# Indirect gathers and scatters that skip empty slots, in a mixture-of-experts kernel on one core

## The chip, the cores and the metric

The kernel runs on 1 core of one Trainium2 chip. The metric is the device time of the whole program in microseconds (us). The engines are named PE (matmul), DVE (vector), ACT (scalar), POOL (GpSimd) and SP (sync, which here only issues transfers). PEld is PE's weight load. All transfers of the core run on the same 16 DMA engines; those that SP issues stand on queue q1, those that POOL issues on queue q0.

## The reference, cut to what matters

One encoder layer on 768 tokens (a sequence of 512 and one of 256) of width 1024, all in float32: a token mixer (differential attention beside retention), then a mixture of experts, then a last RMSNorm. What the change touches is the mixture:

```
e_sel  = top-2 experts of each token, inside its best group      # 32 experts, 768 * 2 = 1536 assignments
h      = silu(x @ w1[e]) * (x @ w3[e])                           # x: 1024, h: 512
y      = h @ w2[e]
out[t] = x2[t] + gate[t, 0] * y[t, 0] + gate[t, 1] * y[t, 1]     # then RMSNorm
```

## The kernel before

The token mixer and the router run in the first 705 us. The router counts the tokens of each expert and cuts each expert's list into blocks of 64 slots (`CAP`). Every expert has at least one block, so there are 32 blocks and one more for each full 64 that an expert exceeds. In this run there are 41 (the groups of the block loop count 41 in the profile). Blocks of one expert follow each other, `served[b]` is the expert of block b, and `nb` is the number of blocks, known only when the router has run. Slots that no token fills stay empty: 41 * 64 = 2624 slots stand for 1536 assignments.

`idxt[p, b]` is an integer that says which half row (512 numbers, 2 KB) partition p of block b wants. Partitions 0 to 63 hold the first halves of the block's 64 rows, partitions 64 to 127 the second halves. It is made by twelve small matmuls (L799) of a slot matrix `Rt` with `Bt`, whose entries are the token's number, and then 2 * token + half (L1537). An empty slot sums to token 0, so it fetches row 0.

The block loop runs on five engines, each in its own program order, joined by semaphores. In block b:

- **POOL** copies column b of `idxt` to `idxb` (L1671), waits for that copy and issues an indirect gather of 128 half rows from `xn_scratch` to the one buffer `xg` (L1674), then waits until `ystage` holds the result of an older block and issues two plain stores of 64 half rows to `y_scratch` (L1681). In its loop the order is gather(b + 2), store(b), then gather(b + 3) and so on, in one queue of instructions.
- **PE** waits for the gather and transposes `xg` to columns (L810), does the down projection of the block before (L841, 16 matmuls), transposes the hidden values (L829), and does the up projection (L820, 32 matmuls).
- **DVE** copies the transposed rows out of PSUM (L1555), forms the hidden values (L1561, L1563) and, when the next block has another expert, copies that expert's w1 and w3 from `rawe` to `cur13a` and `cur13b` (L1577).
- **ACT** does the sigmoid (L1115), copies the result to `ystage` (L1126) after the wait for the older stores, copies the hidden columns (L1120), and, for another expert, copies w2 to `cur2` (L1142).
- **SP** loads the experts' weights into a double buffer (L502), three transfers of 2 MB for each expert: w1 and w3 when DVE has copied the expert two back, w2 when ACT has.

After the last block POOL waits for all stores and issues twelve indirect gathers of 128 rows of 4 KB from `y_scratch` by slot number, two for each tile of 128 tokens (L1698). DVE adds them, scaled by the gates, to `x2` (L1597, L1599), ACT squares and sums (L1152), and the last norm follows (L1155, L1606 on DVE for three tiles, L1705 on POOL for three), then the output stores (L529).

Much earlier, POOL zeroes a small tile and writes the slots of `y_scratch` behind the 32nd block with zeros (L1653), and stores the normalised rows of each tile to `xn_scratch` (L1662).

Of the kernel before, what the change touches and what calls it, by code (L numbers as in the profile page):

```python
# [23 lines left out]
P = 128  # L24
# [15 lines left out]
MAXB = T // CAP  # L40
NOV = (2 * T) // (CAP + 1)
NB = NE + NOV
EW = 12288
EPS = 1e-6
LAM_INIT = 0.8 - 0.6
# [13 lines left out]
_n = 0  # L59
for _name, _w in (("ident", P), ("tri", P), ("ones", P), ("rel", RELW), ("cosA", 32), ("sinA", 32),  # L60
                  ("cosR", 128), ("sinR", 128), ("ecap", NE), ("grank", NG), ("erank", NE),
                  ("iota", P), ("half", 1), ("thr", MAXB - 1), ("tok", NT)):
    _c[_name] = (_n, _n + _w)
    _n += _w
NCST = _n
# [2 lines left out]
def constants():  # L68

    import numpy as np  # L70
    t = np.zeros((P, NCST), np.float32)

    def put(name, v):
        a, b = _c[name]
        t[:, a:b] = v
    i = np.arange(P)
    put("ident", np.eye(P))
    put("tri", (i[:, None] < i[None, :]).astype(np.float32))
    put("ones", 1.0)
# [12 lines left out]
    put("iota", np.arange(P))  # L92
    put("thr", CAP * np.arange(1, MAXB))
    put("half", (i // CAP)[:, None])
    put("tok", i[:, None] + P * np.arange(NT)[None, :])
    return t


def hybrid_layer(nc, A):
# [50 lines left out]
    nbi = small("nbi", [1, 1], I32)  # L150
    served = small("served", [1, NB + 1], I32)
    bcol = small("bcol", [P, 8])
    idxb = small("idxb", [P, 1], I32)
    sdum = small("sdum", [P, 1])
    F_O = off[0]
    FREE = 212800 - F_O
# [6 lines left out]
    zrow = at("zrow", F_O + 36 * KB, [P, 256])  # L163
# [56 lines left out]
    xg = at("xg", D_O + 40 * KB, [P, 512])  # L220
    ystage = at("ystage", D_O + 44 * KB, [P, 512])

    ya = [[at(f"ya{t}{k}", RAW_O + (2 * t + k) * 4 * KB, [P, D]) for k in range(2)] for t in range(NT)]
# [10 lines left out]


    z_d = nc.dram_tensor("z_scratch", [T, D_IN], F32, kind="Internal").ap()
    xn_d = nc.dram_tensor("xn_scratch", [T, D], F32, kind="Internal").ap()
    xn_halves = xn_d.rearrange("t (h n) -> (t h) n", h=2)
    y_d = nc.dram_tensor("y_scratch", [NB * CAP, D], F32, kind="Internal").ap()

    def sem(name):
        return ctx.enter_context(nc.semaphore(name))
    with ctx:
# [100 lines left out]
        s_ys = sem("s_ys")  # L344
        s_md = sem("s_md")
        s_zr = sem("s_zr")
        s_g1 = [sem(f"s_g1{t}") for t in range(NT)]
        s_c2 = sem("s_c2")
        s_sq3 = sem("s_sq3")
# [40 lines left out]
        def _(sp):  # L390
# [90 lines left out]
                    sp.wait_ge(s_lo, ZP + p - 5)  # L481
                    p_piece(p)
            sp.wait_ge(s_mgd, 2 * NT)
            sp.wait_ge(s_ys, 32)
            sp.dma_start(g2[:, :], A["ffn_norm_g"].partition_broadcast(P)[:, 0, :]).then_inc(s_rp, 16)
            sp.dma_start(wrt[:, :, 0:NG], A["w_rg"][0].rearrange("(p c) g -> p c g", c=KC)).then_inc(s_rp, 16)
            for g in range(NG):
# [370 lines left out]
        def _(act):  # L858
# [273 lines left out]
            with act.Fori(1, nb) as b:  # L1132
# [26 lines left out]
        def _(dve):  # L1159
# [377 lines left out]
            link(dve.tensor_scalar(idxt[:, :], ps[4][:, 0:NB + 1], 2.0, C("half"), ALU.mult, ALU.add))  # L1537
            dve.sem_inc(s_nb, 1)

            dve.wait_ge(s_re, 3)  # L1540
# [52 lines left out]
                rsqrt(a, b, D, link)  # L1593
                dve.sem_inc(s_rstd3, 1)
            for t in range(NT):
                dve.wait_ge(s_g1[t], 32)
                link(dve.scalar_tensor_tensor(out=x2[:, t, :], in0=ya[t][0][:, :], scalar=gates[:, 0, t:t + 1],  # L1597
                                              in1=x2[:, t, :], op0=ALU.mult, op1=ALU.add))
                dve.scalar_tensor_tensor(out=x2[:, t, :], in0=ya[t][1][:, :], scalar=gates[:, 1, t:t + 1],  # L1599
                                         in1=x2[:, t, :], op0=ALU.mult, op1=ALU.add).then_inc(s_c2, 1)  # L1600
                if t == 2:
                    last_norm(0, 2)
# [8 lines left out]
        def _(pool):  # L1611
# [34 lines left out]
            silu_steps(1)  # L1646


            pool.memset(zrow[:, :], 0.0).then_inc(s_zr, 1)
            pool.wait_ge(s_zr, 1)  # L1650
            rest = y_d[NE * CAP:NB * CAP, :].rearrange("(e r) (q c) -> (r q) e c", r=32, c=256)
            for u in range(2):
                pool.dma_start(rest[:, u * NOV:(u + 1) * NOV, :],  # L1653
                               zrow[:, :].unsqueeze(1).to_broadcast([P, NOV, 256])).then_inc(s_ys, 16)

            pool.wait_ge(s_hi, ZP + 1)
            pool.tensor_tensor(elo[P_LO[0]][:, :], raw[3][:, :], ehi[P_HI[0]][:, :].bitcast(F32),
                               ALU.subtract).then_inc(s_lo, 1)

            for t in range(NT):  # L1660
                pool.wait_ge(s_rr, t + 1)
                pool.dma_start(xn_d[t * P:(t + 1) * P, :], rrow[t % 2][:, :]).then_inc(s_rst[t % 2], 16)  # L1662

            for k in range(2):
                pool.wait_ge(s_rst[k], 16 * NT // 2)
            pool.wait_ge(s_nb, 1)
            nb = pool.value_load(nbi[0:1, 0:1], min_val=NE, max_val=NB)

            def gather(b):
# [2 lines left out]
                pool.wait_ge(s_ic, b + 1)  # L1672
                pool.sem_inc(s_idx, 1)
                pool.indirect_dma_start(out=xg[:, :], out_offset=None, in_=xn_halves,  # L1674
                                        in_offset=bass.IndirectOffsetOnAxis(ap=idxb[:, 0:1], axis=0)).then_inc(s_gx, 16)

            def store(b):

                pool.wait_ge(s_yc, b + 2)
                for u in range(2):  # L1680
# [9 lines left out]
                gather(b + 2)  # L1690
                store(b)
            store(nb - 1)
            pool.wait_ge(s_ys, 32 * nb + 32)
            pool.wait_ge(s_gx, 16 * nb + 16)
            pool.sem_inc(s_md, 1)
            for t in range(NT):
                for k in range(2):
                    pool.indirect_dma_start(out=ya[t][k][:, :], out_offset=None, in_=y_d,  # L1698
                                            in_offset=bass.IndirectOffsetOnAxis(ap=sloti[:, k, t:t + 1], axis=0)
                                            ).then_inc(s_g1[t], 16)  # L1700

            pool.wait_ge(s_gf, 16)
            for t in range(3):
                pool.wait_ge(s_ym, t + 1)
# [26 lines left out]
```

## Time and profile before

| | |
|---|---|
| median of 3 runs | 1406.74 us (1406.67 to 1407.38) |
| the profiled execution's own time | 1407.34 us |
| its span in the profile | 1405.4 us |
| granted TensorE clock, mean | 0.911 |
| block loop, first gather to last store | 705.56 to 1359.4 us |
| blocks, and blocks that begin another expert | 41, 31 |

The profiled execution agrees with the runs that were timed within 0.6 us. Its span is 1.94 us shorter than its own time, and what lies outside the span is not touched here. The page gives busy shares over the whole span; the block loop takes nearly half of it.

### The profile page before, as it was taken

The page shows a single profiled execution, that of the slowest core. Times are in us where ns is not written, and L with a number is a line of the kernel's source. Part 1 is how long each engine was busy: PE and PEld are TensorE (multiplying, and loading weights), DVE is VectorE, ACT ScalarE, POOL GpSimd, SP SyncE. Part 2 cuts the span into 40 slices and gives each one's busy share as a digit, 9 for nine tenths or more (in the row PEclk, how much of TensorE's full clock was granted, in tenths as well). Part 3 has the DMA queues.
Part 4 walks back from the last instruction along what each step waited for, and adds up shares of the span by engine and source line. Part 5 has one row for each costly group of instructions (what it writes and reads, how often), then busy time and mean ns, then how long its engine had stood idle before and what let it go on. Part 6 is the DMA issues. An engine that isn't in the chain of part 4 may idle for free.

```text
span 1405.4 us, 15836 instructions
## 1 busy us (share of the span) xinstructions
PE 1167.4 (83%) x5178; PEld 697.0 (50%) x5178; DVE 520.6 (37%) x889; ACT 424.7 (30%) x671; POOL 194.0 (14%) x293
## 2 busy tenths in 40 slices
PE   2999999999899779999567888778888888978840
PEld 2788888888666458888522332222233323322210
DVE  3531111115277575643623433333222322234407
ACT  4422222221355563321402233222122121222322
POOL 0011010101070010000011111111111111211134
PEclk9999999999999679999678999999899998999975
DMA  7233332511605045323948999999856587489935
GB/s 278 86 138 112 105 112 107 199 45 48 235 2 173 0 151 182 91 77 142 424 163 322 397 422 421 422 421 422 335 215 238 189 334 277 140 329 422 378 100 214
DMA packets 74047, 311.51 MB, mean 222 GB/s; under 512 B 12576, under 2 KB 12576, under 8 KB 49440
## 3 DMA queue, kind: packets, MB, share of 16 engines
q1 hardware_dynamic: 57824, 258.15, 46.8%
q0 software_dynamic: 16192, 52.97, 10.8%
q8 instruction: 17, 0.28, 0.1%
q14 instruction: 14, 0.11, 0.0%
HBM read 272.29 MB, written 38.80 MB: 221 GB/s over the span
## 4 chain that ended last, share of the span: by engine, by line
PE 63%; DMA 16%; issue 7%; DVE 6%; ACT 4%; POOL 1%; POOLq 1%; SPq 0%; DVEq 0%; ACTq 0%
DMA xg<-xn_scratch,idxb 15%; PE ps L841 13%; PE ps L537 11%; PE ps L539 11%; PE ps L538 11%; PE ps L820 6%; PE ps L810 3%; PE ps L636 1%; ACT ystage L1126 1%; PE ps L657 1%; PE ps L669 1%; PE ps L754 1%; POOL y_scratch L1681 1%; PE ps L648 1%; DVE att L1291 1%
## 5 line engine op out<-in xcount | busy, mean ns | idle before, releaser
L841 PE MATMUL ps<-cur,hT 128*64 128x512 f32 x656 | 191.6, 738 | 4.3 <-ACTq L1145 4.3
L537 PE MATMUL ps<-whi,xTh 128*128 128x512 f32 x480 | 188.5, 393 | 6.2 <-DVE xTl L1228 4.1
L538 PE MATMUL ps<-wlo,xTh 128*128 128x512 f32 x480 | 187.9, 391 | 0.0
L539 PE MATMUL ps<-whi,xTl 128*128 128x512 f32 x480 | 187.8, 391 | 0.0
L1555 DVE COPY xT<-ps 128x512 f32<-128x512 f32 x41 | 28.4, 692 | 422.7 <-PE ps L810 422.7
L820 PE MATMUL ps<-cur13a,xT 128*64 128x512 f32 x656 | 154.2, 612 | 6.2 <-DVEq L1579 5.4
L820 PE MATMUL ps<-cur13b,xT 128*64 128x512 f32 x656 | 148.1, 592 | 0.0
L1172 DVE TENSOR_TENSOR wlo<-raw,whi 128x2048 fp32r<-128x2048 f32 x27 | 61.7, 2292 | 218.2 <-ACT whi L864 218.0
L810 PE MATMUL ps<-cst,xg 128*128 128x128 f32 x168 | 35.9, 345 | 106.5 <-DMA xg<-xn_scratch,idxb 106.4
L1681 POOL DMA_DIRECT2D y_scratch<-ystage x82 | 54.4, 665 | 499.5 <-ACT ystage L1126 498.5
L1126 ACT ACTIVATE ystage<-ps 128x512 f32<-128x512 f32 x41 | 24.5, 598 | 309.8 <-PE ps L841 309.8
L1142 ACT ACTIVATE cur<-rawe 128x4096 f32 x31 | 112.2, 3619 | 0.0
L841 PEld LDWEIGHTS ps<-cur,hT 128*64 128x64 f32 x656 | 53.4, 168 | 113.5 <-issue 110.2
L915 ACT ACTIVATE zst<-ps 128x512 f32<-128x512 f32 x60 | 35.8, 598 | 235.1 <-PE ps L539 235.1
L537 PEld LDWEIGHTS ps<-whi,xTh 128*128 128x128 f32 x480 | 90.8, 189 | 25.4 <-ACT xTh L884 6.8
L539 PEld LDWEIGHTS ps<-whi,xTl 128*128 128x128 f32 x480 | 90.8, 189 | 19.1
L538 PEld LDWEIGHTS ps<-wlo,xTh 128*128 128x128 f32 x480 | 90.8, 189 | 18.9
L810 PEld LDWEIGHTS ps<-cst,xg 128*128 128x128 f32 x168 | 25.3, 211 | 142.2 <-DMA xg<-xn_scratch,idxb 140.6
L820 PEld LDWEIGHTS ps<-cur13b,xT 128*64 128x64 f32 x656 | 50.1, 137 | 90.7 <-issue 90.7
L820 PEld LDWEIGHTS ps<-cur13a,xT 128*64 128x64 f32 x656 | 47.3, 140 | 83.1 <-issue 78.7
L1615 POOL DMA_DIRECT2D z_scratch<-zst x60 | 33.2, 553 | 333.0 <-ACT zst L915 332.9
L1577 DVE COPY cur13a<-rawe 128x4096 f32 x31 | 71.3, 2301 | 7.9 <-issue 7.9
(219 smaller groups left out, 1470.6 us busy)
## 6 DMA issues: line engine op xcount, KB each, us to landing
rawe<-in_w SPq DMA_DIRECT2D x96, 2048.0 KB, 12.1
raw<-in_w_in SPq DMA_DIRECT2D x20, 1024.0 KB, 5.8
z_scratch<-zst POOLq DMA_DIRECT2D x60, 256.0 KB, 2.3
y_scratch<-ystage POOLq DMA_DIRECT2D x82, 128.0 KB
gat<-z_scratch SPq DMA_DIRECT2D x12, 512.0 KB, 4.0
y_scratch<-zrow POOLq DMA_DIRECT2D x2, 2944.0 KB
raw<-in_w_out SPq DMA_DIRECT2D x4, 1024.0 KB, 7.1
xn_scratch<-rrow POOLq DMA_DIRECT2D x6, 512.0 KB, 2.9
```

What stands on the lines that cost most here:

```text
L537: pe.matmul(out, ah, bh, start=first, stop=False)
L538: pe.matmul(out, ah, bl, start=False, stop=False)
L539: return pe.matmul(out, al, bh, start=False, stop=last)
L810: mm = pe.transpose(ps[2][:, c * P:(c + 1) * P], xg[:, c::4], ident)
L820: mm = pe.matmul(ps[0][u * CAP:(u + 1) * CAP, :], xT[:, c, h * CAP:(h + 1) * CAP], cur13[h][:, :, c * 512 + u * 256:c * 512 + u * 256 + 25 ...
L841: mm = pe.matmul(ps[6][u * CAP:(u + 1) * CAP, :], hT[:, k, h * CAP:(h + 1) * CAP], cur2[:, c:c + 512], start=(h == 0 and k == 0), stop=(h ...
L915: act.activation(zst[k][:, :], ps[k][:, :], ACT.Copy).then_inc(s_zev, 1)
L1126: act.activation(ystage[:, :], ps[6][:, :], ACT.Copy).then_inc(s_yc, 1)
L1142: act.activation(cur2[:, :], rawe[:, bass.ds((e % 2) * EW + 4 * PIECE, 2 * PIECE)], ACT.Copy).then_inc(s_cw2, 1)
L1172: dve.tensor_tensor(elo[slot][:, :], raw[slot_raw][:, :], hi[:, :].bitcast(F32), ALU.subtract).then_inc(s_lo, 1)
L1577: dve.tensor_copy(cur13[h][:, :, :], pair[:, :, h * PIECE:(h + 1) * PIECE]).then_inc(s_c13, 1)
L1681: pool.dma_start(y_d[bass.ds(b * CAP, CAP), u * 512:(u + 1) * 512], ystage[u * CAP:(u + 1) * CAP, :]).then_inc(s_ys, 16)
```

## The change

Three things change together. First, the code in `Bt` is now such that a filled slot of block b gives the index 4 * token + 2 * choice + half (at most 3071), while an empty slot gives 4096 or 4097. The gather passes `bounds_check=4 * T - 1` and `oob_is_err=False`, so that it moves nothing for empty slots. For the index to fit, `xn_scratch` holds each row twice, once for each choice. Second, the result of a block is stored by one indirect scatter with the same indices, straight to row (token, choice) of `y_scratch`, where it was two plain stores to the block's place. The scatter needs its own copy of the index column, `idxs`. Third, the twelve indirect gathers at the end become six plain transfers of 1 MB, issued by SP. What belongs to it: the zeroing of unused slots and SP's wait on it go away, `xg` is zeroed once, and ACT's first loop step is taken out of its loop, so that the wait counts stay constant where they must.

```
-    xn_d = nc.dram_tensor("xn_scratch", [T, D], F32, kind="Internal").ap()
-    y_d = nc.dram_tensor("y_scratch", [NB * CAP, D], F32, kind="Internal").ap()
+    xn_d = nc.dram_tensor("xn_scratch", [T, 2, D], F32, kind="Internal").ap()
+    xn_halves = xn_d.rearrange("t k (h n) -> (t k h) n", h=2)
+    y_d = nc.dram_tensor("y_scratch", [T, 2, D], F32, kind="Internal").ap()
+    y_halves = y_d.rearrange("t k (h n) -> (t k h) n", h=2)
...
@@ sync, router's inputs
-            sp.wait_ge(s_ys, 32)
@@ sync, after the weights
             sp.wait_ge(s_md, 1)
+            for t in range(NT):
+                sp.dma_start(ya[t][:, :, :], y_d[t * P:(t + 1) * P, :, :]).then_inc(s_g1[t], 16)
@@ scalar, rows_out
-                act.wait_ge(s_ys, 32 * b + 32)
+                if not (isinstance(b, int) and b == 0):
+                    act.wait_ge(s_ys, 16 * b)
...
-            rows_out(nb - 1)
+            last = act.value_load(nbi[0:1, 1:2], min_val=NE - 1, max_val=NB - 1)
+            rows_out(last)
@@ vector, router
-                                  C("tok")[:, t:t + 1], ALU.is_equal, ALU.mult).then_inc(s_tb, 1)
+                                  C("code")[:, q:q + 1], ALU.is_equal, ALU.mult).then_inc(s_tb, 1)
+            link(dve.tensor_scalar(nbi[:, 1:2], run[0:1, a, Z0 + NE - 1:Z0 + NE], float(NE - 1), None, ALU.add))
...
-            link(dve.tensor_scalar(idxt[:, :], ps[4][:, 0:NB + 1], 2.0, C("half"), ALU.mult, ALU.add))
+            link(dve.tensor_scalar(idxt[:, :], ps[4][:, 0:NB + 1], -2.0, C("half"), ALU.mult, ALU.add))
@@ gpsimd
-                pool.dma_start(xn_d[t * P:(t + 1) * P, :], rrow[t % 2][:, :]).then_inc(s_rst[t % 2], 16)
+                pool.dma_start(xn_d[t * P:(t + 1) * P, :, :], rrow[t % 2][:, :].unsqueeze(1).to_broadcast([P, 2, D])).then_inc(s_rst[t % 2], 16)
...
+            pool.memset(xg[:, :], 0.0).then_inc(s_zr, 1)
+            pool.wait_ge(s_zr, 1)
             pool.wait_ge(s_nb, 1)
@@ gather
-                                        in_offset=bass.IndirectOffsetOnAxis(ap=idxb[:, 0:1], axis=0)).then_inc(s_gx, 16)
+                                        in_offset=bass.IndirectOffsetOnAxis(ap=idxb[:, 0:1], axis=0),
+                                        bounds_check=4 * T - 1, oob_is_err=False).then_inc(s_gx, 16)
@@ store
                 pool.wait_ge(s_yc, b + 2)
-                for u in range(2):
-                    pool.dma_start(y_d[bass.ds(b * CAP, CAP), u * 512:(u + 1) * 512],
-                                   ystage[u * CAP:(u + 1) * CAP, :]).then_inc(s_ys, 16)
+                pool.tensor_copy(idxs[:, :], idxt[:, bass.ds(b, 1)]).then_inc(s_is, 1)
+                pool.wait_ge(s_is, b + 2)
+                pool.sem_inc(s_ids, 1)
+                pool.indirect_dma_start(out=y_halves,
+                                        out_offset=bass.IndirectOffsetOnAxis(ap=idxs[:, 0:1], axis=0),
+                                        in_=ystage[:, :], in_offset=None,
+                                        bounds_check=4 * T - 1, oob_is_err=False).then_inc(s_ys, 16)
@@ end
-            for t in range(NT):
-                for k in range(2):
-                    pool.indirect_dma_start(out=ya[t][k][:, :], out_offset=None, in_=y_d, ...
```

## Rows read from the trace of the kernel before

**Rows 1.** The page: bandwidth in 40 equal slices, and the chain's shares.

```profile
GB/s 278 86 138 112 105 112 107 199 45 48 235 2 173 0 151 182 91 77 142 424 163 322 397 422 421 422 421 422 335 215 238 189 334 277 140 329 422 378 100 214
...
PE 63%; DMA 16%; issue 7%; DVE 6%; ACT 4%; POOL 1%; POOLq 1%; SPq 0%; DVEq 0%; ACTq 0%
```

**Rows 2.** Who waited for whom, in total us, times, longest us.

```profile
PE ps L810 <- DMA xg<-xn_scratch,idxb: 106.4, 31, 7.6
...
POOL idxb L1671 <- DVEq L1538: 27.7, 1, 27.7
```

**Rows 3.** The chain in order of time: start us, length us, what.

```profile
908.45 6.97 DMA xg<-xn_scratch,idxb
916.32 5.15 PE ps L841 x16
924.98 6.88 DMA xg<-xn_scratch,idxb
```

**Rows 4.** POOL in order of time, 889 to 925 us; idle before in brackets.

```profile
889.27 1.91 POOL L1681 DMA_DIRECT2D y_scratch<-ystage  x2 [11.55 <-ACT ystage L1126]
...
906.33 1.12 POOL L1681 DMA_DIRECT2D y_scratch<-ystage  x2 [13.13 <-ACT ystage L1126]
907.44 0.20 POOL L1671 COPY idxb<-idxt 128x1 int32 x1
908.45 1.01 POOL L1674 DMA_INDIRECT xg<-xn_scratch,idxb  x1 [0.81 <-POOL idxb L1671]
```

**Rows 5.** DVE in order of time, beside the first of these stores.

```profile
888.26 2.29 DVE L1577 COPY cur13b<-rawe 128x4096 f32 x1
```

**Rows 6.** The block loop's groups, 705 to 1357 us.

```profile
L1681 POOL DMA_DIRECT2D y_scratch<-ystage x80 | 53.3, 668 | 489.2 <-ACT ystage L1126 488.3
L1674 POOL DMA_INDIRECT xg<-xn_scratch,idxb x42 | 42.3, 1007 | 35.7 <-POOL idxb L1671 33.5 <-issue 2.3
```

**Rows 7.** The instructions of xg: time to landing.

```profile
DMA to landing us min/median/max: 3.1/6.9/7.9
```

**Rows 8.** PE in order of time, four blocks.

```profile
931.91 0.75 PE L810 MATMUL ps<-cst,xg 128*128 128x128 f32 x4 [3.02 <-DMA xg<-xn_scratch,idxb]
932.59 5.35 PE L841 MATMUL ps<-cur,hT 128*64 128x512 f32 x16
...
948.27 0.75 PE L810 MATMUL ps<-cst,xg 128*128 128x128 f32 x4 [2.88 <-DMA xg<-xn_scratch,idxb]
948.95 3.65 PE L841 MATMUL ps<-cur,hT 128*64 128x512 f32 x16
...
1043.41 1.13 PE L810 MATMUL ps<-cst,xg 128*128 128x128 f32 x4 [3.92 <-DMA xg<-xn_scratch,idxb]
1044.46 5.93 PE L841 MATMUL ps<-cur,hT 128*64 128x512 f32 x16
```

**Rows 9.** A window of weight-switching blocks: busy by engine, PEclk, DMA share, GB/s.

```profile
860.00:960.00 100.00, 81.02 (x344) 28.48 (x340) 35.65 (x30) 31.66 (x32) 16.41 (x25) 0.93 1.01 421
```

**Rows 10.** Waits of DVE for what releases the weight copies.

```profile
L1577 DVE COPY cur13a<-rawe 128x4096 f32 x31 | 71.3, 2301 | 7.9 <-issue 7.9
```

**Rows 11.** The end, from the last store: the chain, POOL, SP and DVE.

```profile
1358.84 2.45 DMA y_scratch<-ystage
...
1362.22 1.00 POOL L1698 DMA_INDIRECT ya<-y_scratch,sloti  x1 [2.85 <-DMA y_scratch<-ystage]
...
1361.44 0.35 SPq L523 DMA_DIRECT2D gf<-in_final_norm_g  x1
...
1369.08 1.28 DVE L1597 SCALAR_TENSOR_TENSOR x<-ya,gates,x 128x1024 f32<-128x1024 f32 x1 [26.51 <-DMA ya<-y_scratch,sloti]
```

**Rows 12.** Transfers issued: size of each, median us to landing.

```profile
zv<-z_scratch SPq DMA_DIRECT2D x1, 1024.0 KB, 5.3
...
xn_scratch<-rrow POOLq DMA_DIRECT2D x6, 512.0 KB, 2.9
xres<-in_x_prompt SPq DMA_DIRECT2D x4, 512.0 KB, 3.3
```

More of the change, by code:

```diff
@@ L42 @@
 NB = NE + NOV
+CODES = 1024
 EW = 12288
@@ L61 @@
                   ("cosR", 128), ("sinR", 128), ("ecap", NE), ("grank", NG), ("erank", NE),
-                  ("iota", P), ("half", 1), ("thr", MAXB - 1), ("tok", NT)):
+                  ("iota", P), ("half", 1), ("thr", MAXB - 1), ("tok", 1), ("code", 2 * NT)):
     _c[_name] = (_n, _n + _w)
@@ L93, in constants @@
     put("thr", CAP * np.arange(1, MAXB))
-    put("half", (i // CAP)[:, None])
-    put("tok", i[:, None] + P * np.arange(NT)[None, :])
+    put("half", 4 * CODES + (i // CAP)[:, None])
+    put("tok", i[:, None])
+    q = np.arange(2 * NT)
+    put("code", 2 * CODES - 2 * (i[:, None] + P * (q % NT)[None, :]) - (q // NT)[None, :])
     return t
@@ L149, in hybrid_layer @@
     v6 = small("v6", [P, 9, NT])
-    nbi = small("nbi", [1, 1], I32)
+    nbi = small("nbi", [1, 2], I32)
     served = small("served", [1, NB + 1], I32)
@@ L153, in hybrid_layer @@
     idxb = small("idxb", [P, 1], I32)
+    idxs = small("idxs", [P, 1], I32)
     sdum = small("sdum", [P, 1])
@@ L162, in hybrid_layer @@
     sqx = [at(f"sqx{s}", F_O + (24 + 4 * s) * KB, [P, D]) for s in range(2)]
-    zrow = at("zrow", F_O + 36 * KB, [P, 256])
     lamr = at("lamr", F_O + 36 * KB, [P, 4, HD])
@@ L221, in hybrid_layer @@
     ystage = at("ystage", D_O + 44 * KB, [P, 512])
-    ya = [[at(f"ya{t}{k}", RAW_O + (2 * t + k) * 4 * KB, [P, D]) for k in range(2)] for t in range(NT)]
+    ya = [at(f"ya{t}", RAW_O + t * 8 * KB, [P, 2, D]) for t in range(NT)]
     gf = at("gf", HL_O, [P, D])
@@ L236, in hybrid_layer @@
     z_d = nc.dram_tensor("z_scratch", [T, D_IN], F32, kind="Internal").ap()
-    xn_d = nc.dram_tensor("xn_scratch", [T, D], F32, kind="Internal").ap()
-    xn_halves = xn_d.rearrange("t (h n) -> (t h) n", h=2)
-    y_d = nc.dram_tensor("y_scratch", [NB * CAP, D], F32, kind="Internal").ap()
+    xn_d = nc.dram_tensor("xn_scratch", [T, 2, D], F32, kind="Internal").ap()
+    xn_halves = xn_d.rearrange("t k (h n) -> (t k h) n", h=2)
+    y_d = nc.dram_tensor("y_scratch", [T, 2, D], F32, kind="Internal").ap()
+    y_halves = y_d.rearrange("t k (h n) -> (t k h) n", h=2)
     def sem(name):
@@ L346, in hybrid_layer @@
         s_zr = sem("s_zr")
+        s_is = sem("s_is")
+        s_ids = sem("s_ids")
         s_g1 = [sem(f"s_g1{t}") for t in range(NT)]
@@ L1131, in _, with step @@
             hidden_out(0)
-            with act.Fori(1, nb) as b:
+            def step(b):
                 act.activation(sdum[:, :], cst[:, 0:1], ACT.Sigmoid)
@@ L1145, in _ @@
                 act.sem_inc(s_gc, 1)
-            rows_out(nb - 1)
+            step(1)
+            with act.Fori(2, nb) as b:
+                step(b)
+            last = act.value_load(nbi[0:1, 1:2], min_val=NE - 1, max_val=NB - 1)
+            rows_out(last)
             for t in range(NT):
@@ L1595, in _ @@
             for t in range(NT):
-                dve.wait_ge(s_g1[t], 32)
-                link(dve.scalar_tensor_tensor(out=x2[:, t, :], in0=ya[t][0][:, :], scalar=gates[:, 0, t:t + 1],
+                dve.wait_ge(s_g1[t], 16)
+                link(dve.scalar_tensor_tensor(out=x2[:, t, :], in0=ya[t][:, 0, :], scalar=gates[:, 0, t:t + 1],
                                               in1=x2[:, t, :], op0=ALU.mult, op1=ALU.add))
-                dve.scalar_tensor_tensor(out=x2[:, t, :], in0=ya[t][1][:, :], scalar=gates[:, 1, t:t + 1],
+                dve.scalar_tensor_tensor(out=x2[:, t, :], in0=ya[t][:, 1, :], scalar=gates[:, 1, t:t + 1],
                                          in1=x2[:, t, :], op0=ALU.mult, op1=ALU.add).then_inc(s_c2, 1)
@@ L1646, in _ @@
             silu_steps(1)
-            pool.memset(zrow[:, :], 0.0).then_inc(s_zr, 1)
-            pool.wait_ge(s_zr, 1)
-            rest = y_d[NE * CAP:NB * CAP, :].rearrange("(e r) (q c) -> (r q) e c", r=32, c=256)
-            for u in range(2):
-                pool.dma_start(rest[:, u * NOV:(u + 1) * NOV, :],
-                               zrow[:, :].unsqueeze(1).to_broadcast([P, NOV, 256])).then_inc(s_ys, 16)
             pool.wait_ge(s_hi, ZP + 1)
@@ L1661, in _ @@
                 pool.wait_ge(s_rr, t + 1)
-                pool.dma_start(xn_d[t * P:(t + 1) * P, :], rrow[t % 2][:, :]).then_inc(s_rst[t % 2], 16)
+                pool.dma_start(xn_d[t * P:(t + 1) * P, :, :], rrow[t % 2][:, :].unsqueeze(1).to_broadcast([P, 2, D])).then_inc(s_rst[t % 2], 16)
             for k in range(2):
                 pool.wait_ge(s_rst[k], 16 * NT // 2)
+            pool.wait_ge(s_rr, NT)
+            pool.sem_inc(s_is, 1)
+            pool.memset(xg[:, :], 0.0).then_inc(s_zr, 1)
+            pool.wait_ge(s_zr, 1)
             pool.wait_ge(s_nb, 1)
@@ L1674, in gather @@
                 pool.indirect_dma_start(out=xg[:, :], out_offset=None, in_=xn_halves,
-                                        in_offset=bass.IndirectOffsetOnAxis(ap=idxb[:, 0:1], axis=0)).then_inc(s_gx, 16)
+                                        in_offset=bass.IndirectOffsetOnAxis(ap=idxb[:, 0:1], axis=0),
+                                        bounds_check=4 * T - 1, oob_is_err=False).then_inc(s_gx, 16)
             def store(b):
                 pool.wait_ge(s_yc, b + 2)
-                for u in range(2):
-                    pool.dma_start(y_d[bass.ds(b * CAP, CAP), u * 512:(u + 1) * 512],
-                                   ystage[u * CAP:(u + 1) * CAP, :]).then_inc(s_ys, 16)
+                pool.tensor_copy(idxs[:, :], idxt[:, bass.ds(b, 1)]).then_inc(s_is, 1)
[5 more added lines that the diff above has]
+                                        bounds_check=4 * T - 1, oob_is_err=False).then_inc(s_ys, 16)
             gather(0)
@@ L1692, in _ @@
             store(nb - 1)
-            pool.wait_ge(s_ys, 32 * nb + 32)
+            pool.wait_ge(s_ys, 16 * nb)
             pool.wait_ge(s_gx, 16 * nb + 16)
             pool.sem_inc(s_md, 1)
-            for t in range(NT):
-                for k in range(2):
-                    pool.indirect_dma_start(out=ya[t][k][:, :], out_offset=None, in_=y_d,
-                                            in_offset=bass.IndirectOffsetOnAxis(ap=sloti[:, k, t:t + 1], axis=0)
-                                            ).then_inc(s_g1[t], 16)
             pool.wait_ge(s_gf, 16)
```

## The prediction

> **What bounds the kernel now.** I read the shares of the chain first, then the waits, then the chain and the engines in order of time, and last the bandwidth in windows.
>
> The chain gives PE 63% and DMA 16% of the span [rows 1]. The table of waits says which transfer that is: PE stood still 106.4 us in 31 blocks for the gather into `xg`, 3.43 us each [rows 2]. Nothing waits for weights: DVE's idle time ahead of its 31 weight copies is 7.9 us in all, 0.25 us each, and no DMA is named [rows 10]. So in 31 of 41 blocks a ring sets the time. The chain shows one turn of it: a gather is issued at 908.45 us, takes 6.97 us, PE then transposes and does the down projection (5.15 us), and the next gather starts at 924.98 us, 16.53 us after the first [rows 3]. Between the down projection and that next gather lie the copy to `ystage` and POOL's own program: the pair of stores, 1.12 us, then the index copy, 0.20, a wait of 0.81 for it, and the gather's issue, 1.01 [rows 4]. POOL runs in order, so whatever the store costs it also costs the next gather.
>
> Beside this ring the DMA engines are full: 421 GB/s at a busy share of 1.01 from 860 to 960 us [rows 9], and flat slices of 421 and 422 [rows 1]. A block with new weights needs 3 * 2.1 = 6.29 MB, with gather and stores of 0.26 MB each 6.82 MB, which is 16.2 us at 421 GB/s. The ring's turn is 16.5 us [rows 3]. The two limits are that close, and a second kind of bound has to be kept among the rivals. That the gather takes 6.9 us in the median and 3.1 at least [rows 7] is the price of sharing.
>
> **The change, part by part.**
>
> *The store of a block, on the ring.* Before, 80 plain stores in the window take 668 ns each [rows 6], 1.34 us a block; the mean hides two sizes, 1.12 us and 1.91 us, and the long pair at 889.27 lies over DVE's weight copy that began at 888.26 and takes 2.29 [rows 4, 5]. After, the store is an index copy, a wait for it and one indirect issue. The gather shows all three: 0.20 + 0.81 + 1.01 = 2.02 us [rows 4]. That is +0.68 us a block. Nobody else is queued behind it on POOL but the next gather, and PE waits for that. Over the 31 blocks in which PE waits for the gather: +21.1 us. In the other 10, PE has slack, and I cost it at nothing; without that slack it would be 7 us more. Below the price stands +0.11 us a block if all stores had been of the long kind (3 us in all), above it +0.90 if all had been short (28 us), and 1.3 us more in a block where the small copy must wait for DVE's weight copy to end. The skill speaks of that: the Trainium skill, "DMA: Bandwidth & Descriptors", section on SWDGE vs HWDGE vs iDMA, says that descriptors issued by GpSimd are written into on-chip rings from which VectorE's fast copy mode can shut GpSimd out. The long pairs agree, 1.91 against 1.12 us.
>
> *The gather moves fewer rows.* 1536 of 2624 slots are filled, 58.5%, so 41% of the 256 KB fall away. No trace row shows a gather with holes. From below: at 421 GB/s the 256 KB take 0.62 us, 41% of it is 0.25 us; and if holes cost what rows cost, it is 0. From above: were all that a shared gather takes over the quickest one proportional to its rows, it would be 0.41 * (6.9 - 3.1 + 0.62) = 1.8 us [rows 7]. I take 0.5 us, near the lower end, because the quickest gather already spends 2.5 of 3.1 us on something that isn't data, and a first row that has to wait for weight packets waits as long with few rows as with many. That gives 31 * 0.5 = -15.5 us. By the Trainium skill's fit in "DMA: Bandwidth & Descriptors", section on the anatomy of one DMA (a fixed 2 us, and bytes at 436 GB/s), an estimate is 0.25 us a gather, and the whole sum would end some 8 us higher than mine.
>
> *The scatter moves fewer rows too.* No one waits for it on the ring: ACT's wait for it comes a whole turn later. Zero. The same 41% less on both takes 0.22 MB a block off the DMA engines, which counts only if they are the bound (a rival below).
>
> *TensorE's clock.* After a wait of 3.02 us the down projection takes 5.35 us, after one of 2.88 us it takes 3.65, and after 3.92 us it takes 5.93 [rows 8]. The same 16 matmuls at a lower granted clock cost up to 2.3 us. My net of +0.18 us a block lengthens waits that are on the edge: I count two blocks that lose 1.7 us, +3 us. It can be 0, and +7 if the four blocks whose waits lie near 2.9 us all lose it.
>
> *Ahead of the loop.* DVE has one more instruction on a single element; the smallest copy here takes 0.20 us [rows 4], so +0.2 us at most, and I count it. The doubled store of `xn_scratch` is 1 MB instead of 512 KB, 2.9 us to landing before [rows 12], and clearing `xg` is one POOL instruction; both lie in the 27.7 us in which POOL waits for the router [rows 2]. Without that cover they would be some 3 us. The zeroing that goes away, 5.9 MB or 14 us of bandwidth, ran where the slices show far less than 421 GB/s [rows 1]; I cost it at 0, and at 1 us of gain at most.
>
> *The end.* The last pair of stores landed at 1358.84 + 2.45 = 1361.29 us, the first of the twelve gathers went out at 1362.22, and DVE began at 1369.08 [rows 11]. After: the last scatter is issued 1.01 us later than the stores were (copy and wait), at 1359.3, and lands 3.1 us on [rows 7], at 1362.4. SP, which issued its `gf` load 0.15 us after that moment before, sends the first 1 MB at 1362.6. A transfer of 512 KB lands in 3.3 us and one of 1 MB in 5.3 beside others [rows 12]; 3.3 us and 0.5 MB more at 421 GB/s are 4.5 us, so DVE begins at 1367.1, 2.0 us earlier. The next ones come every 2.5 us and DVE needs two steps of 1.28 us for each, so DVE then sets the pace as it did. -2.0 us, between -3 and -1.
>
> The sum: +21.1 - 15.5 + 3 + 0.2 - 2.0 = +6.8 us on the profiled execution's own 1407.34 us, whose span is 1405.4. The runs' median lies 0.6 us lower, so I forecast 1413.5 us.
>
> **The rivals.**
>
> *Holes save the gather nothing.* A gather has landed when its fullest share has. If the filled rows of a block leave one DMA engine with as many rows as before, or a hole still costs a row's turn, the 15.5 us are lost, and the edge waits go with them: 21.1 + 7 + 0.2 - 2 = +26 us, 1433 us. For it: the rows of a block are filled from the front, so holes are never spread evenly. Against it: half-empty blocks are common at 58.5%. The Trainium skill, same page, section on the descriptor swizzle, gives each engine fixed partitions, 0 to 3 and 32 to 35 for the first. By it, a block with 36 or more of its 64 slots filled gains nothing, and one with at most 32 halves the fullest engine. No trace row here names the engine of a row.
>
> *Faster through the clock.* If the gather lands over 0.85 us earlier, more than the store costs, the waits of 3.0 us fall below 2.9 and the clock stays up: with 1.0 us saved, 31 * -0.32 = -10, twelve of the blocks save 1.7 us more, -20, and the end -2: 1375 us. For it: the waits of 2.88 and 3.02 us stand 0.14 us apart, with 1.7 us between their outcomes [rows 8]. It decides from 0.85 us saved a gather. Against it: 1.0 us is four times what bandwidth alone gives.
>
> *Faster through bandwidth.* If the DMA engines and not the ring set the turn (16.2 against 16.5 us, share 1.01), 0.22 MB less are 0.52 us less for each of some 24 blocks in the full stretches, -12.5, the store's price is hidden, and the end gives 2: 1392 us. For it: the closeness of the two numbers. Against it: nothing waits for weights [rows 10].
>
> **How the numbers follow.** This kernel's measurement can tell 0.2%, 2.8 us. The forecast case, 1409.6 to 1425 us, gets 0.40; holes that save nothing, 1425 to 1445, 0.22; terms that cancel within 0.2%, 0.12; bandwidth, 1390 to 1404, 0.12; the clock, below 1390, 0.14. So faster 0.26, same 0.12, slower 0.62. The range of 1391 to 1437 us leaves out most of the clock's case and the top of the first rival's. The forecast case's own range is 1408 to 1425.
>
> **What would show it.** Right: the time from the copy to `ystage` to the next gather's issue grows by some 0.7 to 0.9 us; the gather's median landing falls from 6.9 to about 6.4; the turn of 16.5 us grows to 16.7; from the last landing of results to DVE's first step of the end it takes 4.7 us, where it was 7.8. Wrong: landings of 6.9 (first rival), down projections of 3.65 us in most blocks (the clock), turns near 15.7 us with waits of DVE on weights (bandwidth), or an indirect issue with bounds that takes much else than 1.01 us, which would move the sum by 62 times the difference.

## The result, and the profile after

The changed kernel takes 1457.16 us (median of 4 runs) where the kernel before takes 1407.06: ratio 1.0363, 95% interval 1.0323 to 1.0403. It is 50 us slower. I had forecast 1413.5 us and a range up to 1437.

The page of the changed kernel, the answer to [rows 1]:

```profile
GB/s 279 102 112 109 109 100 194 102 50 50 210 1 1 1 237 137 94 116 349 249 287 363 386 365 402 370 389 341 204 190 193 187 310 219 93 301 367 377 59 232
...
PE 57%; DMA 19%; issue 9%; DVE 6%; ACT 5%; POOL 2%; POOLq 1%; SPq 0%; DVEq 0%; ACTq 0%
```

The flat slices of 421 and 422 GB/s are gone. Fewer bytes move, 299.47 MB instead of 311.51, over a longer span. The chain has more DMA (19%, was 16%) and more issue time, and less PE. The table of waits, the answer to [rows 2], and the groups of the block loop, the answer to [rows 6]:

```profile
PE ps L816 <- DMA xg<-xn_scratch,idxb: 148.4, 37, 9.1
```

```profile
L1684 POOL DMA_INDIRECT xg<-xn_scratch,idxb x42 | 46.0, 1096 | 37.2 <-POOL idxb L1681 34.9 <-issue 2.3
L1694 POOL DMA_INDIRECT y_scratch<-ystage,idxs x41 | 41.8, 1020 | 36.2 <-POOL idxs L1691 36.2
...
L1691 POOL COPY idxs<-idxt 128x1 int32 x41 | 24.8, 606 | 495.0 <-ACT ystage L1133 495.0
```

PE's waits for the gather grew by 42.0 us, from 106.4 in 31 blocks to 148.4 in 37. The scatter's issue takes 1.02 us, as expected. The index copy in front of it does not take what was expected: 606 ns in the mean, for one number a partition. POOL and DVE in order of time show why, beside [rows 4, 5]:

```profile
897.64 1.84 POOL L1691 COPY idxs<-idxt 128x1 int32 x1 [10.44 <-ACT ystage L1133]
900.37 1.01 POOL L1694 DMA_INDIRECT y_scratch<-ystage,idxs  x1 [0.88 <-POOL idxs L1691]
901.38 0.20 POOL L1681 COPY idxb<-idxt 128x1 int32 x1
902.42 1.05 POOL L1684 DMA_INDIRECT xg<-xn_scratch,idxb  x1 [0.85 <-POOL idxb L1681]
```

```profile
897.16 2.29 DVE L1590 COPY cur13b<-rawe 128x4096 f32 x1
```

The small copy starts at 897.64 us, inside DVE's weight copy (897.16 to 899.45), and ends at 899.48, when that has ended. Ten of the 41 copies in this trace take over 1 us. ACT's copy to `ystage` gives the way on POOL its beginning. First the kernel before, then the changed one:

```profile
888.00 0.60 ACT L1126 ACTIVATE ystage<-ps 128x512 f32<-128x512 f32 x1 [6.92 <-PE ps L841]
...
905.05 0.60 ACT L1126 ACTIVATE ystage<-ps 128x512 f32<-128x512 f32 x1 [8.99 <-PE ps L841]
```

```profile
896.88 0.60 ACT L1133 ACTIVATE ystage<-ps 128x512 f32<-128x512 f32 x1 [6.87 <-PE ps L847]
...
1033.75 0.60 ACT L1133 ACTIVATE ystage<-ps 128x512 f32<-128x512 f32 x1 [9.57 <-PE ps L847]
```

From the start of `ystage` to the next gather's issue it took 3.40 us before (905.05 to 908.45, [rows 4]) and takes 3.88 after (1033.75 to 1037.63). Where DVE's weight copy overlaps, it took 4.20 us (888.00 to 892.20) and takes 5.54 (896.88 to 902.42). So a block pays +0.48 us, or +1.34 us where the copy meets DVE's in both kernels.

That is not yet 50 us: 41 times 0.48 and ten times 0.86 more are 28 us, before anything that the change saves is taken off. The starts of the gathers show where the time went. The table gives the time between the starts of gathers 3, 19, 34 and 41, counted from 0:

| us | 3 to 19, weights switch | 19 to 34, mostly two blocks or more an expert | 34 to 41, weights switch |
|---|---|---|---|
| before | 261.2 | 219.2 | 111.9 |
| after | 271.7 | 251.2 | 119.2 |

These three stretches grow by 49.8 us. (The span grows by 48.8: gather 3 starts 3.9 us later, and behind gather 41 the new kernel gains 4.8.) Of the 49.8 us, 32.0 lie in the 15 blocks in the middle: 2.1 us a block, more than either price above. Among gathers 19 to 33, 7 were issued over 5 us before PE's transposition in the kernel before, and 13 in the changed one. The six new ones are gathers 20, 22, 24, 27, 30 and 32. From each of them to the next gather it took 11.7 to 12.6 us before and takes 15.9 to 18.3 after, 27.9 of the 32.0 us together. One such gather of either kernel, with SP's next weight load and PE; first before:

```profile
1023.53 1.01 POOL L1674 DMA_INDIRECT xg<-xn_scratch,idxb  x1 [0.81 <-POOL idxb L1671]
...
1024.61 0.37 SPq L502 DMA_DIRECT2D rawe<-in_w  x1
...
1027.38 0.74 PE L810 MATMUL ps<-cst,xg 128*128 128x128 f32 x4
1028.06 3.65 PE L841 MATMUL ps<-cur,hT 128*64 128x512 f32 x16
```

and after:

```profile
1037.63 1.05 POOL L1684 DMA_INDIRECT xg<-xn_scratch,idxb  x1 [0.85 <-POOL idxb L1681]
...
1038.20 0.37 SPq L506 DMA_DIRECT2D rawe<-in_w  x1
...
1044.28 0.75 PE L816 MATMUL ps<-cst,xg 128*128 128x128 f32 x4 [3.21 <-DMA xg<-xn_scratch,idxb]
1044.96 5.29 PE L847 MATMUL ps<-cur,hT 128*64 128x512 f32 x16
```

Both times the w2 load goes out when ACT has copied w2, some 4.5 us after `ystage` began, whatever POOL does. The gather was 1.08 us ahead of it and is now 0.57 us ahead; from here on this is called the gather's lead over the load. PE had the rows 3.85 us after the issue without waiting at all; now it has them after 6.65 us, waits 3.21 us, and then runs its down projection in 5.29 us instead of 3.65. The mean granted clock of the middle stretch is 0.90 and was 0.92. The experiments test whether the lost lead is the cause.

The end, the answer to [rows 11], in the chain:

```profile
1409.99 2.36 DMA y_scratch<-ystage,idxs
1412.41 0.04 issue
1412.50 4.84 DMA ya<-y_scratch
1417.36 1.30 DVE x L1610
```

From the start of the last store on POOL (1408.93 us) to the end of the span (1454.2) it takes 45.3 us, where it was 47.2.

### The profile page after: what moved, and what is told of

Read it like the earlier page. It is cut to its first block, busy times and chain, and to the rows that moved or that the text cites. A ratio compares the mean times of both kernels' runs of the same rounds, so it can differ in the third digit from the quotient of the medians.

```text
span 1454.2 us, 15827 instructions
## 1 busy us (share of the span) xinstructions
PE 1177.2 (81%) x5178; PEld 699.6 (48%) x5178; DVE 520.0 (36%) x890; ACT 424.1 (29%) x671; POOL 195.2 (13%) x279
## 2 busy tenths in 40 slices
DMA packets 71791, 299.47 MB, mean 206 GB/s; under 512 B 14000, under 2 KB 14000, under 8 KB 46416
## 4 chain that ended last, share of the span: by engine, by line
PE 57%; DMA 19%; issue 9%; DVE 6%; ACT 5%; POOL 2%; POOLq 1%; SPq 0%; DVEq 0%; ACTq 0%
DMA xg<-xn_scratch,idxb 18%; PE ps L847 13%; PE ps L543 11%; PE ps L545 11%; PE ps L544 10%; PE ps L816 3%; PE ps L826 2%; POOL idxs L1691 2%; ACT ystage L1133 2%; PE ps L642 1%; PE ps L663 1%; PE ps L675 1%; PE ps L760 1%; DVE x L1612 1%; DVE x L1610 1%
## 5 line engine op out<-in xcount | busy, mean ns | idle before, releaser
L847 PE MATMUL ps<-cur,hT 128*64 128x512 f32 x656 | 198.1, 760 | 4.3 <-ACTq L1153 4.3
L816 PE MATMUL ps<-cst,xg 128*128 128x128 f32 x168 | 37.8, 360 | 148.6 <-DMA xg<-xn_scratch,idxb 148.4
L1133 ACT ACTIVATE ystage<-ps 128x512 f32<-128x512 f32 x41 | 24.5, 597 | 358.9 <-PE ps L847 358.9
L847 PEld LDWEIGHTS ps<-cur,hT 128*64 128x64 f32 x656 | 55.3, 175 | 119.6 <-issue 116.9
L1691 POOL COPY idxs<-idxt 128x1 int32 x41 | 24.8, 606 | 495.0 <-ACT ystage L1133 495.0
```

Source lines behind the costliest of these rows:

```text
L816: mm = pe.transpose(ps[2][:, c * P:(c + 1) * P], xg[:, c::4], ident)
L847: mm = pe.matmul(ps[6][u * CAP:(u + 1) * CAP, :], hT[:, k, h * CAP:(h + 1) * CAP], cur2[:, c:c + 512], start=(h == 0 and k == 0), stop=(h ...
L1691: pool.tensor_copy(idxs[:, :], idxt[:, bass.ds(b, 1)]).then_inc(s_is, 1)
```

## The experiments

Theory 1: the longer way on POOL, and what a later gather runs into. Theory 2, the rival: the indirect transfers with bounds and holes are slow in themselves. Ratios are to the kernel before, measured beside each variant; times of different variants that were not measured side by side are better compared by these ratios.

**b_delay and b_skip** put one part of the change each into the kernel before.

```
b_delay:         pool.wait_ge(s_yc, b + 2)
+                pool.tensor_copy(idxs[:, :], idxt[:, bass.ds(b, 1)]).then_inc(s_is, 1)
+                pool.wait_ge(s_is, b + 1)
                 for u in range(2): ...
b_skip (the new index codes and the zeroing of xg are left out here):
...
+                                        bounds_check=2 * T - 1, oob_is_err=False).then_inc(s_gx, 16)
```

> The kernel before, with one thing added: ahead of each pair of plain stores POOL copies the index column and waits for the copy, as the changed kernel does. No hole is skipped, nothing is scattered, the end is the old one. Theory 1 (the longer way on POOL from ystage to the next gather is the cause, and what it costs is more than itself, because the gather then starts too late to be ahead of the next weight load): the loop grows as in the changed kernel, some +1.2 us a block, and the time is 1450 to 1462 us. Theory 2 (the indirect transfers with bounds and holes are what is slow): only the delay itself shows, 0.5 us in each of 31 to 41 blocks, 1422 to 1428 us.

> The kernel before, with the gather alone changed: empty slots get an index out of bounds and are skipped; stores, scratch layout and end are the old ones. Theory 1: skipping costs nothing and saves about 0.3 us a landing in the blocks that wait; 1394 to 1408 us. Theory 2: the skipping gather is slower to issue or to land; 1420 us or more.

b_delay took 1446.37 us, ratio 1.0292 (1.0267 to 1.0318): an index copy that nothing uses costs 41 us. That is a little under its range. b_skip took 1395.42 us, ratio 0.9933 (0.9905 to 0.9960): skipping alone is a gain of 10 us. That is theory 1. From `ystage` to the gather the copy adds 0.34 us (3.75 against 3.41), 14 us in 41 blocks, and some 0.85 us more in the 15 blocks in which it took over 1 us: 27 us at most, so the delay costs more than itself. Skipping shortened the median landing from 6.9 us [rows 7] to 6.5:

```profile
DMA to landing us min/median/max: 2.2/6.5/7.6
```

**b_small and a_small** take the competition away: only 64 of each half's 2048 weight columns are loaded for experts 2 to 31. Most of the weights are left out, so the result is not the layer's.

```
...
+                    sp.dma_start(rawe[:, c:c + 2 * PIECE].rearrange("p (h n) -> p h n", h=2)[:, :, 0:64],
+                                 e_w[k][bass.ds(e, 1)][0][:, :, 0:64]).then_inc(done[par], 16)
```

> The kernel before with the weight loads of experts 2 to 31 cut to 64 of 2048 columns a half (most of the weights are left out, so the result is not the layer's). It takes the competition away from the gather. Theory 1: landings of 3 to 4 us in all blocks, hardly a wait of PE for a gather, loop near 41 * 12.4 us, 1255 to 1275 us. Theory 2 says the same of this kernel.

> The changed kernel with the same cut of the weight loads (most of the weights are left out). Theory 1: with nothing to compete with, 0.5 us on POOL's way is covered by PE's own work, and the kernel is within 6 us of the kernel before with the same cut. Theory 2: scatter and skipping gather keep their price, 20 us or more over it.

Single executions: 1272.88 us before, 1297.34 us changed. The first is as expected, the second is not: I expected PE's own work to cover the difference. The waits of both, the kernel before first:

```profile
PE ps L814 <- DMA xg<-xn_scratch,idxb: 10.9, 14, 6.0
```

```profile
PE ps L820 <- DMA xg<-xn_scratch,idxb: 37.6, 32, 5.5
```

Without heavy loads the changed kernel's gather lands in 3.1 us (median; 3.5 in b_small) and nothing of it should show. But here PE runs at full clock (granted clock 1.00 in windows from 760 to 1100 us), its down projection takes 3.65 us in every block, `ystage` comes early, and so the index copy falls on DVE's weight copy in 30 of 41 blocks instead of 10:

```profile
973.31 1.84 POOL L1695 COPY idxs<-idxt 128x1 int32 x1 [7.64 <-ACT ystage L1137]
```

So the direct price of the change, without any competition, is 24.5 us, and some 26 with the 2 us that the end gives back. By what I had written above, "20 us or more" speaks for theory 2; the next runs decide between the two.

**a_hoist and a_hoist1** take the index copies off the way. Both make the scatter's copy ahead of the wait for `ystage`; a_hoist makes the gather's there as well.

```
-                pool.wait_ge(s_yc, b + 2)
+                if not (isinstance(b, int) and b == 0):
+                    pool.wait_ge(s_ys, 16 * b)
                 pool.tensor_copy(idxs[:, :], idxt[:, bass.ds(b, 1)]).then_inc(s_is, 1)
                 pool.wait_ge(s_is, b + 2)
+                pool.wait_ge(s_yc, b + 2)
                 pool.sem_inc(s_ids, 1)
...
```

> The changed kernel with both index columns (of the scatter and of the next gather) copied while POOL waits for ystage, so that behind ystage only the two indirect issues are left. Theory 1 (the way on POOL between ystage and the next gather sets the cost, the small copy waiting for DVE's weight copy above all): that way falls from 3.1 to 4.8 us to 1.6 to 1.9 us, below the 2.1 to 2.9 us of the kernel before, and the time is 1365 to 1392 us. Theory 2 (scattering itself, or its bounds, is slow): it stays over 1410 us.

> The changed kernel with only the scatter's index column copied ahead of the wait for ystage; the gather's own index copy stays behind the scatter, where it has always been. If the new index copy on the ring is the whole cause, the way from ystage to the next gather is that of the kernel before, and the time is 1390 to 1402 us. If the small copy that waits for DVE's weight copy merely moves from idxs to idxb, it stays at 1410 to 1435 us.

a_hoist took 1397.16 us, ratio 0.9947 (0.9926 to 0.9968), 5 us over its range; a_hoist1 took 1405.96 us, ratio 0.9985 (0.9970 to 0.9999), between its two ranges. With the scatter's copy moved ahead of a wait, the same scatter, the same skipping and the same end are as fast as the kernel before. Theory 2 has fallen. In the trace of a_hoist1 the lead of gathers 20, 24, 27, 30 and 32 is back at 0.91 to 0.93 us, and PE has their rows after 3.7 to 4.0 us. The scatter now follows `ystage` directly, and in a_hoist, whose lines these are, the gather follows the scatter:

```profile
962.97 1.03 POOL L1701 DMA_INDIRECT y_scratch<-ystage,idxs  x1 [7.21 <-ACT ystage L1133]
964.31 1.04 POOL L1689 DMA_INDIRECT xg<-xn_scratch,idxb  x1 [0.31 <-issue]
```

**a_full, after_again, a_full_again** ask what skipping is worth in the changed kernel. The empty slots get the index of a spare row instead of one out of bounds.

```
-CODES = 1024
+CODES = T
...
-                                        bounds_check=4 * T - 1, oob_is_err=False)      # gather and scatter
```

> The changed kernel without any skipping: empty slots get the index of a spare row, which the gather reads and the scatter writes like any other. It gives what skipping alone is worth in the changed kernel. Both theories of the delay: skipping saves what it saved in the kernel before, 0.3 us a landing and some races, so this is 8 to 20 us slower than the changed kernel, 1465 to 1477 us. If holes cost what rows cost, it is the same, 1457 us.

> The changed kernel as it is, beside the next one, to tell what skipping is worth in it: 1452 to 1462 us.

> The changed kernel without skipping, empty slots going to a spare row. It took 1448.9 us where 1465 or more was expected. If skipping is a loss in the changed kernel, it is 6 us or more faster than the kernel beside it; if the two are the same within what separate runs tell, 1452 to 1460 us.

a_full took 1448.93 us where I expected 1465 or more. Side by side the changed kernel took 1459.41 us, ratio 1.0365 (1.0351 to 1.0379), and a_full_again 1448.91, ratio 1.0300 (1.0279 to 1.0321). The intervals are apart: in the changed kernel skipping costs 10 us, where in the kernel before it saved 10. The stretches of a_full are 271.5, 243.7 and 119.6 us: the difference lies in the middle again. There the gather is 0.71 us ahead of the load, because the way from `ystage` to the gather is 0.14 us shorter without the bounds (3.75 us, where the changed kernel takes 3.88):

```profile
1039.27 0.20 POOL L1684 COPY idxb<-idxt 128x1 int32 x1
1040.27 1.00 POOL L1687 DMA_INDIRECT xg<-xn_scratch,idxb  x1 [0.80 <-POOL idxb L1684]
...
1040.98 0.37 SPq L507 DMA_DIRECT2D rawe<-in_w  x1
...
1045.43 0.75 PE L817 MATMUL ps<-cst,xg 128*128 128x128 f32 x4 [1.58 <-DMA xg<-xn_scratch,idxb]
```

PE has the rows 5.16 us after the issue, between 3.85 and 6.65.

**b_delay_late, a_late, a_full_late** test the lead itself. Nothing is taken off POOL's way; ACT makes one more copy, and the w2 load waits for it.

```
...
+                with act.If(e > e0):
+                    act.activation(slow[:, :], cst[:, 0:D], ACT.Copy).then_inc(s_late, 1)
...
-                    sp.wait_ge(s_cw2, e - 1)
+                    sp.wait_ge(s_late, e - 1)
```

> The kernel before with the index copy and its wait ahead of the plain stores (as b_delay, which took 41 us more than before), and ACT does one more copy of 128x1024 behind its w2 copy, after which alone SP may issue the next w2 load (and the loads queued behind it): that load goes out some 1.1 us later. Theory of the lost lead (in blocks of the same expert the gather used to go out 1.1 us ahead of the w2 load and landed in 3.9 us, and a gather that is 0.5 us later loses that lead and takes 5 to 8): the lead comes back and with it most of the loss in the 17 blocks in the middle; 1412 to 1430 us. Rival (only the ring's own length counts): 1443 to 1452 us, as b_delay.

> The changed kernel (1459 us in its last runs) with SP's w2 loads made to go out some 1.1 us later, by the extra ACT copy of b_delay_late. In the changed kernel a gather goes out 0.57 us ahead of the w2 load and lands after 6.3 to 7.5 us; without skipping 0.71 us ahead, 5.2 to 5.5 us; in the kernel before 1.08 us ahead, 3.85 us. Theory of the lead: with some 1.7 us of lead all of those land in 3.9 us or less, and this is 1418 to 1436 us. If skipping has a cost of its own that has nothing to do with the lead, it stays 10 us above a_full_late.

> The same without skipping (1449 us without the extra copy). Theory of the lead: with the lead won in both, skipping is worth what it was in the kernel before, so this is 3 to 15 us slower than a_late beside it; the sign of the difference turns round. Otherwise it stays faster by some 10 us.

b_delay_late took 1422.15 us, ratio 1.0108 (1.0091 to 1.0124), against 1446.37 for b_delay. a_late took 1417.21 us, ratio 1.0075 (1.0059 to 1.0090), against 1459.41, and is 1 us below its range. The load comes later, ACT does more, and 42 us are back (41 by the ratios). a_full_late took 1425.41 us, ratio 1.0124 (1.0105 to 1.0143): with the lead won in both kernels, skipping is a gain again, 8 us. In a_late POOL, SP and PE show the gather 1.82 us ahead and no wait:

```profile
1090.34 1.05 POOL L1689 DMA_INDIRECT xg<-xn_scratch,idxb  x1 [0.85 <-POOL idxb L1686]
...
1092.16 0.37 SPq L508 DMA_DIRECT2D rawe<-in_w  x1
...
1093.71 0.75 PE L818 MATMUL ps<-cst,xg 128*128 128x128 f32 x4
```

These 42 us are not all the price of the lost slack. In the traces of after_again and a_late the middle stretch falls from 252.1 to 232.8 us, 19.3 us, and is still 13.6 us longer than before. The two stretches in which weights switch give the other 22.6 us, and the first is at 257.9 us shorter than in the kernel before (261.2). There too the later load lets gathers through early: gathers 4, 9 and 13 reach PE after 3.4 to 3.5 us in a_late, after 6.6 to 7.6 in the changed kernel and after 7.0 to 7.4 in the kernel before. So the experiment shows that the lead decides when the rows come, and the size of the loss in the middle is read from the traces of before and after.

The table gives the lead over the w2 load, and the time from the gather's issue to PE's transposition, for the gathers of the middle stretch that have such a load behind them. In the rows of 3.4 to 4.0 us PE mostly did not wait, so that the rows were there earlier still. Gather 28 is left out in every row: three loads went out in the block before it, and it takes 5.2 us in b_delay and 6.6 to 8.4 us in the others, whatever its own lead.

| kernel | lead, us | rows at PE after, us |
|---|---|---|
| b_delay_late | 1.74 to 1.99 | 3.4 to 3.6 |
| a_late | 1.80 to 1.82 | 3.4 to 3.5 |
| before | 0.82 to 1.09 | 3.8 to 4.0 |
| a_hoist1 | 0.91 to 0.93 | 3.7 to 4.0 |
| b_skip (once) | 0.76 | 4.6 |
| b_delay | 0.73 | 4.7 to 5.2 |
| a_full | 0.70 to 0.71 | 4.9 to 5.5 |
| after | 0.57 to 0.58 | 5.8 to 6.7 |
| b_delay (twice) | 0.49, 0.50 | 7.4, 6.9 |
| after, a_late (once each) | 0.37 | 7.6, 7.9 |

**b_early, a_early, a_full_early** take the store off the ring: the next gather goes out before the older block's store.

```
...
-                pool.wait_ge(s_tx, b + 2)
-                pool.wait_ge(s_gx, 16 * b + 32)
-                gather(b + 2)
+                pool.wait_ge(s_tx, b + 3)
+                pool.wait_ge(s_gx, 16 * b + 48)
+                gather(b + 3)
                 store(b)
...
```

> The kernel before with POOL's order changed alone: gather(b + 3) goes out before store(b), as soon as PE has transposed the block before. It takes the store and its way off the ring. Theory 1: PE hardly waits for gathers; the turn is that of the DMA engines where weights switch (24 blocks at 16.2 us) and PE's own 12.3 us in the other 17, 1345 to 1365 us. If the DMA engines had been the bound all along, nothing moves: 1400 us or more.

> The changed kernel with the same order. Theory 1: the store's longer way no longer matters, fewer bytes do: 24 blocks at 15.7 us, 17 at 12.3, the end 2 us shorter, 1330 to 1355 us, the same as or up to 15 us faster than the kernel before with that order. Theory 2: slower than that one by 20 us or more.

> The changed kernel with the gather issued ahead of the older store, and no skipping. a_early (with skipping) took 1329.9 us, b_early 1339.9 us. If the 10 us between these two are the end (2 us) and fewer bytes on full DMA engines in the weight-switching blocks, this one is at 1336 to 1341 us.

b_early took 1339.85 us, ratio 0.9532 (0.9503 to 0.9561); a_early 1329.87 us, ratio 0.9465 (0.9435 to 0.9496); a_full_early 1337.40 us, ratio 0.9506 (0.9492 to 0.9521). The first is 5 us faster than its range, the second is at the lower end of its own, the third lies in its own. a_early is the fastest version of this study, 76 us faster than the kernel before, and it contains the whole change. Its windows, and what DVE waited for:

```profile
860.00:960.00 100.00, 79.31 (x336) 30.13 (x338) 38.92 (x32) 33.25 (x32) 32.73 (x26) 0.93 1.01 420
980.00:1100.00 120.00, 118.68 (x546) 43.90 (x542) 38.23 (x42) 32.74 (x46) 43.24 (x41) 1.00 0.79 308
```

```profile
DVE cur13a L1590 <- DMA rawe<-in_w: 51.7, 19, 4.2
```

Where weights switch, DVE now waits for weights with the DMA engines full; in the middle PE is busy 118.68 of 120 us. Skipping is worth 6 to 8 us here (a_early against a_full_early, by the ratios or by the times; they were not measured side by side, and their intervals overlap at the edge). In the traces 5.3 us of it lie where weights switch (240.5 and 97.0 us, where a_full_early has 244.0 and 98.8) and nothing in the middle (178.0 both). That is under half of the 0.52 us a block that the rival of bandwidth counted on.

## Why the prediction was wrong

*The store's price.* Forecast +0.68 us a block from a mean. Measured +0.48 us, and +1.34 where the copy meets DVE's weight copy. I had named that case ("1.3 us more in a block where the small copy must wait") as an upper end. It was ten blocks in the changed kernel, and it was 30 of 41 with small loads. Without competition the sum, 24.5 us plus the 2 us of the end, comes near the 21.1 us forecast, but by luck: it is made of other blocks and other prices.

*The step that failed* is "In the other 10, PE has slack, and I cost it at nothing". I took slack against a fixed landing time. Most of the slack blocks had their rows after 3.85 us only because their gather went out some 1.08 us ahead of a 2 MB load, and the store sits in front of that gather. At 0.57 us ahead they became waiting blocks (31 before, 37 after), and with the wait came a slower down projection, 4.7 to 5.8 us in the six of the middle instead of 3.65. The traces give the size. Ten gathers between 3 and 40 had been at PE within 4.6 us in the kernel before, with no wait of PE or one under 0.7 us (5, 20, 22, 24, 25, 27, 30, 32, 33, 35). From these to the next gather the time grew by 37.6 of the 49.8 us of the loop; over the other 28 it grew by 12.2 us, where my terms for the waiting blocks came to 8.6. The experiments move the loss with the lead in both directions: b_delay takes it away without any of the rest of the change, a_hoist1 and a_late give it back. The trace of before held what would have shown it: the gather at 1023.53 and the load at 1024.61.

*The gather's fewer rows.* Forecast -15.5 us. Measured -10 us in the kernel before (b_skip), +10 us in the changed one, -8 us once the lead is restored. The mechanism was right and the size near; the sign in the changed kernel was not, for 0.14 us on POOL's way against a lead that was already short. I had also taken 3.1 us [rows 7] for the quickest gather; it is the one behind the last block, whose rows nobody uses, and the quickest of a real block took 3.4 us. My first rival, holes that save nothing, is not what happened: b_skip lands at 6.5 us in the median. Its 1433 us was the nearest of my cases, for a wrong reason. Which DMA engine the rows of a block go to was not tried, so the rule on fixed partitions stays open.

*TensorE's clock.* Forecast +3 us. The 656 matmuls of the down projection take 198.1 us instead of 191.6, +6.5 us. Right in kind, twice the size. My edge between waits of 2.9 and of 3.0 us does not hold: the changed kernel has 5.35 us after a wait of 2.36, and the kernel before has 3.65 after one of 3.08. What else decides it was not tried. First the changed kernel, then the kernel before:

```profile
1248.30 0.75 PE L816 MATMUL ps<-cst,xg 128*128 128x128 f32 x4 [2.36 <-DMA xg<-xn_scratch,idxb]
1248.97 5.35 PE L847 MATMUL ps<-cur,hT 128*64 128x512 f32 x16
```

```profile
1279.20 0.75 PE L810 MATMUL ps<-cst,xg 128*128 128x128 f32 x4 [3.08 <-DMA xg<-xn_scratch,idxb]
1279.88 3.65 PE L841 MATMUL ps<-cur,hT 128*64 128x512 f32 x16
```

*Ahead of the loop.* +0.2 us forecast; the first gather goes out at 706.94 instead of 705.56 in this trace, and at 706.1 in a second one. By gather 3 the delay is 3.9 us (2.4 in the second trace). No run takes this apart.

*The end.* -2.0 us forecast, -1.9 measured; DVE begins 5.0 us after the scatter's landing where I had put 4.7, and the scatter lands 2.4 us after its issue where I had put 3.1.

*The two rivals on the faster side.* The clock case needs earlier gathers and had none, and by the line above on waits its condition was not one to rely on. The bandwidth case was wrong for this kernel, for DMA share fell to 0.95 and 383 GB/s from 860 to 960 us, but it is what bounds the reordered kernels where weights switch.

## What to carry to other kernels

When a change makes a transfer later, look not only at who waits for it, but at what large transfer is issued just behind it, and how long its lead is; a lead of half a microsecond can be worth more than the work that is saved. A tiny operation on POOL is not tiny while DVE makes a wide copy, so index columns belong ahead of a wait, not behind it. And before making a step on a ring cheaper, ask whether it has to be on the ring: a store in front of a gather that doesn't need it was worth 66 us.

## What the runs showed of the hardware

- A POOL copy of 128x1 took 0.18 us by itself and 1.84 us when it began 0.48 us into DVE's 128x4096 copy; it ended within 0.03 us of that copy's end. An indirect issue took 1.0 to 1.1 us in most blocks; the longest gather issue took 2.92 us in the changed kernel, and the longest scatter issue 4.54 us in a_early.
- An indirect gather landed 2.6 to 4.0 us after its issue when SP's 2 MB load was issued 0.82 us or more behind it and nothing older was in flight, was at PE after 4.6 to 5.6 us with 0.70 to 0.76 us between them, after 5.8 to 6.8 us with 0.56 to 0.58 us, and after 6.9 to 7.9 us with 0.50 us or less. Why the step is so steep was not tried.
- Skipped rows do leave the DMA engines: a_full moved 308.63 MB, the changed kernel 299.47, and the quickest landing of a block's gather was 2.8 us with skipping, 3.4 without (3.3 in a_full). The gather behind the last block has no filled slot: in the changed kernel it moved no rows and landed after 2.2 us, where it took 3.1 before [rows 7].
- An indirect issue with a bounds check took 1.05 us against 1.00 in a_full, and the wait ahead of it 0.85 us against 0.80.
